# Interleaving U-row gathers with GpSimd splits, and running a block's cast half first on TensorE

## What is computed

```python
def peer_ffn(x, w_q, sub_keys, u, v):
    def chunk(xc):
        q = (xc @ w_q).reshape(c, PEER_HEADS, 2, PEER_HALF_DIM)
        sc = jnp.einsum('chpd,hpnd->chpn', q, sub_keys, preferred_element_type=jnp.float32)
        top_s, top_i = lax.top_k(sc, kk)
        cand = top_s[:, :, 0, :, None] + top_s[:, :, 1, None, :]
        cand_s, cand_i = lax.top_k(cand.reshape(c, PEER_HEADS, kk * kk), kk)
        ...
        experts = i1 * PEER_N_KEYS + i2
        gates = jax.nn.softmax(cand_s, axis=-1)
        ue = jnp.take(u, experts, axis=0)
        ve = jnp.take(v, experts, axis=0)
        act = jax.nn.gelu(jnp.einsum('chkd,cd->chk', ue, xc), approximate=False)
        return jnp.einsum('chk,chkd->cd', gates.astype(xc.dtype) * act, ve)
```

## Time and profile before

| what | us |
|---|---|
| three timed runs | 3535.57, 3535.60, 3549.32 |
| their median | 3535.6 |
| the profiled execution: its own time | 3530.59 |
| its span (first to last instruction) | 3529.0 |

### The profile page before, as it was taken

How to read it: one execution, slowest core, us unless ns; L and a number is a source line. 1 busy time by engine, 2 the same in 40 slices (tenths; PEclk the granted TensorE clock), 3 DMA queues, 4 the chain that set the end, 5 groups by cost and what they waited for, 6 DMA issues and landing times.

```text
span 3529.0 us, 67255 instructions
## 1 busy us (share of the span) xinstructions
PE 3294.9 (93%) x18452; PEld 2961.4 (84%) x18454; DVE 2491.6 (71%) x5419; ACT 1367.2 (39%) x2110; POOL 1956.2 (55%) x1558
## 2 busy tenths in 40 slices
PE   8999898889999899999899998989899998999996
PEld 8888788888999788888688887888889988888885
DVE  1454554888787688898924545458887877889898
ACT  2354244444433333333324542444444333333332
POOL 3434346777654266666544342467776543666664
PEclk9999999999999999999999999999999999999998
DMA  4001137888788599999820011378887985999996
GB/s 159 25 1 60 48 103 230 285 283 287 248 257 260 161 335 323 338 339 337 306 86 25 1 60 54 111 233 287 282 284 248 270 251 169 347 337 337 339 336 231
DMA packets 402485, 765.11 MB, mean 217 GB/s; under 512 B 162400, under 2 KB 261472, under 8 KB 398432
## 3 DMA queue, kind: packets, MB, share of 16 engines
q1 hardware_dynamic: 197088, 462.06, 39.0%
q0 software_dynamic: 73728, 268.47, 20.8%
q10 hardware_dynamic: 131584, 33.56, 4.5%
HBM read 677.98 MB, written 85.98 MB: 216 GB/s over the span
## 4 chain that ended last, share of the span: by engine, by line
PE 55%; issue 21%; POOL 11%; DVE 5%; DMA 3%; ACTq 3%; ACT 1%; POOLq 1%; DVEq 1%; SPq 0%
PE ps L1717 24%; POOL st_lo L608 6%; PE ps L1451 6%; PE ps L1452 6%; PE ps L1453 6%; PE ps L1684 4%; PE ps L1573 3%; POOL u_row L619 3%; PE ps L1550 3%; ACTq L934 2%; PE ps L1558 2%; DMA h_in<-gelu_d 2%; PE ps L1539 1%; DMA st_raw<-in_peer_v 1%; DMA u_row<-in_peer_ur,idx_u 1%
## 5 line engine op out<-in xcount | busy, mean ns | idle before, releaser
L608 POOL TENSOR_TENSOR st_lo<-st_raw,st_hi 128x1024 fp32r<-128x1024 f32 x290 | 695.5, 2399 | 632.2 <-ACT st_hi L857 628.7
L1451 PE MATMUL ps<-t_hi,st_hi 128*128 128x384 f32 (+1 forms) x2304 | 822.5, 357 | 83.7 <-POOL st_lo L608 80.3
L857 ACT CAST st_hi<-st_raw 128x1024 fp32r<-128x1024 f32 x544 | 570.4, 1048 | 747.6 <-PE ps L1717 462.6
L1453 PE MATMUL ps<-t_hi,st_lo 128*128 128x384 f32 (+1 forms) x2304 | 801.3, 348 | 0.0
L1452 PE MATMUL ps<-t_lo,st_hi 128*128 128x384 f32 (+1 forms) x2304 | 801.2, 348 | 0.0
L717 POOL TENSOR_TENSOR wt_lo<-w_f,wt_hi 128x384 fp32r<-128x384 f32 x256 | 420.4, 1642 | 312.5 <-ACT wt_hi L959 311.1
L1451 PEld LDWEIGHTS ps<-t_hi,st_hi 128*128 128x128 f32 x2304 | 440.3, 191 | 130.7 <-POOL st_lo L608 96.1
L1452 PEld LDWEIGHTS ps<-t_lo,st_hi 128*128 128x128 f32 x2304 | 440.6, 191 | 10.5
L1453 PEld LDWEIGHTS ps<-t_hi,st_lo 128*128 128x128 f32 x2304 | 439.5, 191 | 11.4
L1717 PE MATMUL ps<-st_hi,wt_hi 128*128 128x512 f32 x1536 | 390.4, 389 | 5.3 <-ACT wt_hi L959 5.3
L1717 PE MATMUL ps<-st_lo,wt_hi 128*128 128x512 f32 x1536 | 389.8, 389 | 0.0
(11 more groups left out here) (194 smaller groups left out, 5102.6 us busy)
## 6 DMA issues: line engine op xcount, KB each, us to landing
st_raw<-in_peer_u SPq DMA_DIRECT2D x256, 512.0 KB
st_raw<-in_peer_v SPq DMA_DIRECT2D x256, 512.0 KB
gelu_d<-h_out SPq DMA_DIRECT2D x256, 192.0 KB
h_in<-gelu_d SPq DMA_DIRECT2D x256, 192.0 KB
gates_d<-g_stage ACTq DMA_DIRECT2D x32, 1024.0 KB
g_in<-gates_d SPq DMA_DIRECT2D x256, 128.0 KB
w_raw<-in_w_in SPq DMA_DIRECT2D x16, 1168.0 KB, 5.4
st_raw<-in_peer_w_q SPq DMA_DIRECT2D x32, 512.0 KB
```

The source lines that it names most:

```text
L608: nc.gpsimd.tensor_tensor(st_lo[:, s].rearrange("p c f -> p (c f)"), st_raw[:, s], st_hi[:, s].rearrange("p c f -> p (c f)").bitcast(F32), ...
L857: nc.scalar.copy(st_hi[:, s].rearrange("p c f -> p (c f)"), st_raw[:, s]).then_inc(st_h, 1)
L1451: nc.tensor.matmul(dst, lhs[0], rhs[0], start=first, stop=False)
L1453: return nc.tensor.matmul(dst, lhs[1], rhs[0], start=False, stop=last)
```

## The change

Two edits. The plan of GpSimd becomes 4 rounds, first block 6, 26 splits: 6.5 splits for eight gathers, beginning with U block 6 and not 14. Round 0 is spread like the others, without the waits for earlier dots. The three zones hold U blocks 6 to 83; blocks 84 to 89 follow without gathers.

On TensorE `stationary` waits for the cast alone (`st_h`), runs the 16 products that use `st_hi`, then waits for the split (`st_l`) and runs the 8 products that use `st_lo`. It serves the query blocks and all U blocks. The V blocks have code of their own, which is as it was.

```diff
-ZONE_R, ZONE_B0, ZONE_BN = 2, 14, 12
+ZONE_R, ZONE_B0, ZONE_BN = 4, 6, 26
...
-            def zone(z, rounds, done):
-
-                for r in rounds:
-                    for k in round_u(ZONE_R * z + r, r % 2):
+            def zone(z, first=False):
+
+                done = 0
+                for r in range(ZONE_R):
+                    for k in round_u(ZONE_R * z + r, r % 2, first and r == 0):
                         while done * ZONE_R * URING < (URING * r + k + 1) * ZONE_BN - ZONE_BN // 2:
                             rest_block(z * (ZONE_BN // 2) + QB // 2 + (ZONE_B0 + done) // 2, done % 2)
                             done += 1
...
-            for k in round_u(0, 0, first=True):
-                pass
-            done = 0
-            while done * ZONE_R < ZONE_BN:
-                rest_block(QB // 2 + (ZONE_B0 + done) // 2, done % 2)
-                done += 1
-            zone(0, range(1, ZONE_R), done)
+            zone(0, first=True)
             with pool.Fori(1, U_ROUNDS // ZONE_R) as z:
-                zone(z, range(ZONE_R), 0)
+                zone(z)
...
             def stationary(m, s, dst, rows, operand=None):
 
-                pe.wait_ge(st_l[s], ST_PER // 2 * l + m + 1 + 1)
+                pe.wait_ge(st_h, ST_PER * l + 2 * m + s + 1)
                 for c in range(DC):
                     if operand is not None:
                         split_chunk(operand, c)
-                    last = product(dst, (st_hi[:, s, c], st_lo[:, s, c]), (t_hi[:, c, rows], t_lo[:, c, rows]), c == 0,
-                                   c == DC - 1)
+                    nc.tensor.matmul(dst, st_hi[:, s, c], t_hi[:, c, rows], start=c == 0, stop=False)
+                    nc.tensor.matmul(dst, st_hi[:, s, c], t_lo[:, c, rows], start=False, stop=False)
+                pe.wait_ge(st_l[s], ST_PER // 2 * l + m + 1 + 1)
+                for c in range(DC):
+                    last = nc.tensor.matmul(dst, st_lo[:, s, c], t_hi[:, c, rows], start=False, stop=c == DC - 1)
                 last.then_inc(st_used, 1)
```

## The result

| | before | after |
|---|---|---|
| median of runs, us | 3535.6 | 3490.8 |
| lowest and highest of the undisturbed runs, us | 3530.4 to 3549.3 | 3488.5 to 3492.7 |
| profiled execution, us | 3530.6 | 3488.9 |
| its span, us | 3529.0 | 3487.1 |

The ratio is 0.9864, with a 95% interval of 0.9842 to 0.9886: 44.8 us less by the medians, 41.9 by the spans. The changed kernel had four runs; one of them took 6586.6 us, 3.1 ms above the other three, and is left out of the ratio; the median of 3490.8 counts it, and that of the other three is 3488.9. The forecast was 3482, with a range of 3425 to 3525.

The account below looks back on a forecast made before the run. TensorE, 93% busy, was taken as the bound, its waits for splits as the winnable time. The slot loop at 4.7 us a block gave 26.8 us a layer, 53.6 for two: 3477 profiled, 3482 as median, range 3425 to 3525.

Parts of the forecast that it names:

- The mechanism: TensorE's cast half hides gathers ahead of splits (2.8 us slack); casts' waits for U loads then bound, staying at 60 us or more.
- The loop's terms: Split end, hop, transfer, cast, hop, gather, split in a U slot: 4.2 us beside a 5.2 us transfer, 9.4 in all.
- the ring: The same loop through a U slot, setting the zone's pace at 4.7 us a block, above TensorE's 4.22.
- The 5.2 us: Mean U transfer from issue to cast in the zone, taken above the middle of bounds 4.2 and 5.85.
- the rival *Slower: Denser stream lengthens transfers at the load issued at a split's end; mean above 5.9 us, 3552 at 6.1; chance 0.08.
- The blocks behind the zone: Five blocks before the transposes lose their small starts: 23.3 to 21.3 us, 2.0 gained a layer.
- its undisturbed round of 28.4 us: VectorE's 12 rounds from 526.0 end at 867, gates at 878, covered by 34 us before TensorE arrives at about 912.
- The V stage of layer two: The V stage should stay as it is in length.
- The whole sum: 24.8 us from the zone plus 2.0 behind it is 26.8 a layer, 53.6 for two layers.
- transfers have room: Rival: mean transfer falls to 4.4 us or less, TensorE paces the zone at about 4.3 us, 3420; chance 0.28.
- The two rivals at and above the time of before: No notable gain, mean transfer near 5.85 us, 3513 to 3535, chance 0.14; or slower, above 5.9 us, chance 0.08.

Follow-up runs that it names:

- 3: Changed kernel with U loads released by ScalarE's cast instead of the split, st_lo left zero: 3410.2 us, ratio 0.9653 against the kernel before.
- 5: Changed kernel, complete, with each split in two instructions and each U load in two transfers: 3455.9 us, ratio 0.9765; second set 3451.8 us.
- 9: Changed kernel, complete, with splits, U loads and casts all in halves: 3410.0 us, ratio 0.9645 against the kernel before.
- 8: Changed kernel with eight semaphore increments on SP before each U load but a layer's first four: 3550.7 us, ratio 1.0025 against the kernel before.
- 2: Changed kernel with TensorE's old order of products, so GpSimd's edit alone: 3523.0 us, ratio 0.9973 against the kernel before.
- experiment 10: The changed kernel again, unaltered, for how much one execution varies: 3496.1 us, ratio 0.9885 against the kernel before.
- 4: Changed kernel with U gathers of 512 columns, half the bytes, and dots over 512: 3404.3 us, ratio 0.9634 against the kernel before.

## Why the prediction was right, and where its terms were off

**The mechanism held.** TensorE's wait for `st_lo` ended (80.3 to 2.1 us), the casts' wait for U loads was to stay at 60 us or more and rose to 237.4, and the first dot came at 524.9, forecast 526.0. TensorE's longest wait for a cast is 3.5 us, and the longest stall near 560 us is 2.7 (at 567.1). Releasing the load sooner (3, 5, 9) speeds the zone up, releasing it later (8) slows it down, and GpSimd's edit alone hardly moves it (2).

**The loop's terms.** Matching the U loads, casts and splits of layer one's timeline in order (76 of 78 blocks), the mean from issue to cast is 5.33 us, with what a cast waits for TensorE in it (forecast 5.2), the hop from split end to issue 0.23 (0.2), and from a cast's end to its split 0.62, where 0.08 + 0.45 was taken. The loop is 9.6 us and not 9.4, 4.8 a block, 0.1 above the forecast 4.7. That is the mis-sized term: 78 x 0.11 = 8.9 us in layer one, 15.9 gained and not 24.8. In layer two it was 27.1, mean 21.5 a layer; in experiment 10, the same kernel, 19.1 and 16.9.

That these terms add up to two blocks proves nothing by itself. The end of a split issues the slot's next load, so issue to cast, cast and split fill two blocks in any kernel that releases the slot so, with the waiting for TensorE inside them. The proof is in the experiments that change the ring. By the landing marks (67 of layer one's 78 loads have them) the loads of the changed kernel land after 5.1 us in the mean, and in 47 of the 67 blocks the cast begins within 0.2 us of it; in the other 20 it stands behind TensorE's block. The ring is the bound of seven blocks in ten, not of all.

**The 5.2 us came true in part by luck.** It was a choice between two bounds, not read from a row. In the kernel before, matched the same way, issue to cast takes 5.7 us, and the load itself lands after 4.7; the cast stands behind TensorE for the rest. Now the loads land later (5.1 and 4.8 us in the two layers), the way the rival *Slower* pointed, and the cast hardly waits behind them (0.3). The two moves met near the number chosen.

**What a stall costs beyond itself.** The zone stands 375.5 - 78 x 4.22 = 46 us above TensorE's floor. The waits in it add up to 29.4, and to 32.1 with the 2.70 in front of block 84, with which it ends. Of the other 14, some 11 go with the clock: it was granted at 0.97 over the zone, and 3% of 375 us are 11. After 5 of the 12 stalls inside the zone the first product took 0.59 to 0.69 us and its followers came 0.32 us apart and not 0.176, as at 898.14 behind it. Most of the last 3 is in how a wait is counted: from the end of the last product, 0.34 us after its start, where a follower would have started after 0.176, so each of the 15 waits hides 0.17 us. In layer two the clock hardly fell, though its stalls were as long (up to 3.5 us), and that zone was 11.6 us shorter; why it fell in one layer and not in the other is open. In experiments 4 and 9, without such stalls in the zone, the granted clock is 1.00 and the zone is at its floor. The forecast goes by the ring's length and not by a sum of waits, so no term was missing for this. Whoever adds up waits finds 32.1 us of the 46.

**The blocks behind the zone** were to gain 2.0 us and lost 1.1: 25.2 from block 84 to the transposes against 24.15, since block 84 now starts behind a stall at half the clock, with 0.2 us more at the gates. In layer two they lost 0.6.

**VectorE** ended its last round at 901.25, not at 867:

```profile
524.91 1.22 DVE L1287 CUSTOM_DVE_ANT_0 u_row<-ps,u_row 128x1024 f32<-128x1024 f32 x1 [13.88 <-DMA u_row<-in_peer_ur,idx_u]
...
901.25 0.16 DVE L1300 TENSOR_TENSOR dots<-dot,ps 128x8 f32 x1 [0.42 <-DVE i_all L1260]
```

I took its undisturbed round of 28.4 us, but gathers stand between splits and splits follow the loop: a round is 6.5 blocks x 4.81 = 31.3 us, 12 of them from 524.9 end at 900.5. With the 11.3 us to the gates that is 912.6, so TensorE was covered by 10 us at 923, not by 34. It was enough, and no term changed.

**The V stage of layer two was to stay as it was.** From its first product to the end it took 3487.1 - 2929.66 = 557.4 us, against 3529.0 - 2978.89 = 550.1; experiment 10 gave 552.9. The first two windows of 60 us show it:

```profile
2929.00:2989.00 60.00, 56.18 (x243) 45.41 (x244) 43.52 (x52) 18.95 (x26) 36.86 (x31) 1.00 0.91 324
2989.00:3049.00 60.00, 57.38 (x252) 46.88 (x251) 48.93 (x56) 21.66 (x30) 38.74 (x32) 1.00 0.90 317
```

Before, the same two windows had 59.11 and 60.00 us of TensorE. The transposes of layer two came 49.0 us sooner and the end only 41.9; these 7.3 us are why. The twelve profiles of the kernels after and of the experiments, all with the same work in the V stage, have 550.4 to 562.6 us for it, also where TensorE's order is that of before (562.6 in experiment 2). So it varies between executions by more than 7.3 us. With a single profile of before it can't be said whether the change has a part in it.

**The whole sum, by spans:** 41.9 us and not 53.6. The two zones gained 43.0 of the 49.6 forecast. The blocks behind them lost 1.7 and were to gain 4.0. The V stage of layer two lost 7.3, and everything else gained 7.9, 4.1 of it between layer one's first V product and layer two's first U block. The last two had been put at about nothing and they cancel, which is luck.

**The rivals.** That transfers have room, at 3420, was wrong: the casts' waits rose. The Trainium skill's rule (DMA: Bandwidth & Descriptors, Anatomy of one DMA), by which 512 KB take 3.2 us as an estimate, is given there for transfers that GpSimd issues, and SyncE issues these. The quickest load of the zone landed after 3.3 us, near it, but the mean was 5.1 and the longest 8.3, so it doesn't describe loads beside the gathers. With half the gathers' bytes (4) the casts hardly waited. The two rivals at and above the time of before would have needed a mean of 5.85 or more.

## What to carry to other kernels

Where a buffer's release, its load and its use form a ring, the ring's length over the number of slots is a pace like any engine's. Once the compute engine's own wait is gone, that pace is the next bound, and moving gathers between the splits hardly changed it here. What did was to release, refill and cast the slot in halves (81 us), and it should be looked for where casts or splits wait for loads while the DMA engines still have a share free (0.84 here). To size such a ring, read each of its terms from the trace, the landing apart from the wait behind it, and take into account that the loads are uneven. Let the rounds of a covered engine follow the pace of whoever feeds it.

## What the runs showed that I had not expected

- The loads' lateness is uneven: the mean from issue to cast is 5.33 us, a single one 8.4, and TensorE's waits in layer one's zone come as 12 stalls of 1.35 to 2.85 us in 78 blocks, not as a little at each.
- Halving the gathers' bytes was worth 87 us, and TensorE then ran 330.0 of 330 us.
- Splitting GpSimd's subtraction in two costs little (2 x 1300 ns against 2411). With both operands the same block it took 1896 ns.
- A delay of 0.5 us at one issue a block took the whole gain of the change away in the medians (3550.7 us), though the profiled execution kept a part of it (span 3520.0).
